# First loads of three phases issued in the phase before them, in a two-layer recurrent decoder step

## Chip, cores and metric

One core of one Trainium2 chip runs one program. The metric is the device time of one execution in microseconds (us), lower is better.

## What is computed

One inference step of a decoder trunk with two layers, for a prompt of 2048 tokens and a sample group of 8 sequences of 8 tokens, width 1024, all in float32. Cut from the reference:

```python
# every layer
x <- x + gate(c) * RMSNorm_post(mixer(RMSNorm_pre(x) * (1 + scale(c)) + shift(c)))

def mixer_ab(h, ...):      # layer 0: GLA (4 heads) and retention (4 heads)
    gq, gk, gv, gz, glr, rq, rk, rv, rz = split(h @ w_in)
    log_a = log_sigmoid(glr @ w_gate_up + b_gate) / GLA_TAU
    q_r, k_r = rotary(rq), rotary(rk)
    o, s = chunked_gated_linear_attn(q, k, v, log_g, s0)     # S = diag(exp(g)) S + k v^T
    return (norm(o) * silu(z)) @ w_out, s

def mixer_c(h, ...):       # layer 1: gated delta rule, 8 heads
    qkv, z, b_raw, a_raw = split(h @ w_in)
    qkv = silu(causal_conv_of_width_4(qkv))
    q, k = l2norm(q), l2norm(k)
    o, s = chunked_gated_delta(q, k, v, sigmoid(b_raw), log_g, s_delta)
    return (rms_norm(o) * silu(z)) @ w_out, s
```

The outputs are the new tokens and the new states.

## The kernel before

The program is four phases one behind the other. Names of a phase's tiles begin with its short name: `inab` (first projection, with the adaLN conditioning, `phase_in_ab`), `mixab` (layer 0's recurrence and output projection, `phase_mix_ab`), `inc` (second projection and convolution, `phase_in_c`), `mixc` (delta rule and last output projection, `phase_mix_c`). A phase ends with `ph.end()`: the semaphores are cleared and all engines meet at a barrier, so nothing of a phase starts before the last work of the one before is done. Between phases the results go through arrays in device memory (`tmp_qk`, `tmp_v`, `tmp_z`, `tmp_dec` to `mixab`; `tmp_x` to `inc`; `tmp_qkv`, `tmp_z`, `tmp_col`, `tmp_brow` to `mixc`).

Each engine has an instruction stream written out by hand: PE (matmuls), ACT, DVE, POOL, and SP, which only issues DMAs. DMAs are issued from SP's queue and from ACT's. Every wait is a semaphore count. The order of the work around the change is thus the order of the code.

The two projections go in four blocks of 512 prompt tokens and the 64 sample tokens. A block has its normed, transposed tokens in one of two operand rooms: `keep` and a second one of 16 KB per partition, which is `inab_h` in `inab` and `raw_next` in `inc` (allocated in `mixab`, where the class `Early`, L1218, fills it with layer 1's first block; `inc` uses it for blocks 0 and 2). `outputs` (L739 in `inab`) stores a block's results from SP; the last things on SP's queue in `inab` are the stores of block 3 and of the sample (L751 to L768).

The mix phases go in 16 tiles of 128 tokens and one of the sample. Each loads a tile two ahead (`load_tile`, L1382 and L2357) into buffers 0 and 1. SP loads tile 0 first of all, behind the barrier, then the constant tables (`load_tables`, L172, one DMA for each table, from one array in which they lie side by side), then tile 1 and the weights. PE waits for the tables (`tab_in`) at the start of every phase, since the identity matrix for transposes is one of them. In `mixc` ACT issues the load of tile 0's `qkv` (L2579) and SP everything else; ACT's second step waits for the norm weights `gn` (L2381), the last of SP's first loads.

At the tail of `mixab`, layer 1's conditioning is worked out beside the sample tile: `Cond.pair` (L260) multiplies 2 MB pieces of `w_ada`, which ACT loads into a ring of three buffers `cw` (L228), and `Early` squares and norms token tiles (L1234 to L1249).

`inc` converts its 33 weight units of 128 columns while block 0 runs, with the class `Weights` (L530): ACT's queue loads a unit in f32 to one of two stages (L547), ACT rounds it to f16 (`hi`, L556) and POOL subtracts for the remainder (`lo`, L562); each conversion first issues the load of the next unit. A block has 36 groups: 24 of convolution channels, 8 of `z`, 4 of the small columns. A z group needs four units at once. PE multiplies a group into one of four banks, ACT copies it out (`evac`, L1996), DVE convolves (L2085 to L2091), ACT stores. In group g of block 0 ACT and POOL also convert unit 4 + g:

```python
                if first:
                    weights.hi(act, AHEAD + g)      # L2020; AHEAD = 4
```

so unit 27, which the first z group needs, comes in slot 23. The convolution's coefficients (`conv_c`) are loaded by SP as rows (L1886), transposed by PE (L2155) and copied by ACT (L1977) before the first product.

## Time and profile before

| | |
|---|---|
| runs (3), us | 2666.85, 2667.93, 2664.86; median 2666.85 |
| profiled execution, us | 2668.84, span 2667.1 |
| mean granted TensorE clock | 0.965 of full speed |
| PE busy | 2482.0 us (93%) |
| DVE busy | 1320.2 us (50%) |
| ACT busy | 926.3 us (35%) |
| POOL busy | 796.3 us (30%) |
| DMA | 270.37 MB, mean 101 GB/s |

The device time holds a little more than the span, which runs from the first to the last instruction. An engine's busy share is a mean over phases with different limits. SP's and ACT's DMA issues, marked q in the rows, don't count as busy. A row of a timeline gives the start, the duration, the engine, the line and operation, the tile written and those read, the count, and in brackets the idle time ahead with what ended it. The clock of a window is a share of 2.4 GHz, and 0.50 is the lower level of 1.2 GHz.

### The profile page before, as it was taken

To read this page: it belongs to the slowest core of one execution; us is meant where nothing else is said; L and a number is where in the kernel's file an instruction comes from. 1 tells how busy PE (TensorE), PEld (TensorE's weight loads), DVE (VectorE), ACT (ScalarE), POOL (GpSimd) and SP (SyncE) were. 2 spreads that over 40 slices of the span, in tenths; PEclk is the share of its full clock that TensorE was granted. 3 is DMA by queue.
4 is the path that set the end of the run, shared out by engine and by line. 5 is a ranking of instruction groups with operands and counts; after the bars stand their busy time and mean duration, and the time that the engine had idled before them with its cause. 6 is when DMAs were issued, how large, how long until landed. Compare 5 with 4: busy or idle time off the path is not lost. (4 is left out here: it accounts for less than half of the span.)

```text
span 2667.1 us, 53838 instructions
## 1 busy us (share of the span) xinstructions
PE 2482.0 (93%) x21052; PEld 1495.8 (56%) x21052; DVE 1320.2 (50%) x2927; ACT 926.3 (35%) x2664; POOL 796.3 (30%) x848
## 2 busy tenths in 40 slices
PE   7999999997899986989999999985899999999998
PEld 2444444444566632434444444455788787887876
DVE  3412112111687743981643626424666566665666
ACT  3534242322111113432322322234445454554541
POOL 2531001021111103551010000005555556465564
PEclk8999999998999996989999999997999999999998
DMA  8451212033544543542121111116513222231213
GB/s 294 132 157 48 83 45 75 32 117 124 209 146 157 173 162 114 162 135 77 64 72 52 64 52 52 56 48 174 136 58 107 63 81 89 65 105 57 81 46 92
DMA packets 256585, 270.37 MB, mean 101 GB/s; under 512 B 31223, under 2 KB 189959, under 8 KB 256378
## 3 DMA queue, kind: packets, MB, share of 16 engines
q1 hardware_dynamic: 184858, 217.28, 25.1%
q10 hardware_dynamic: 71520, 50.13, 6.7%
q8 instruction: 155, 2.54, 0.4%
q14 instruction: 52, 0.43, 0.1%
HBM read 180.00 MB, written 87.36 MB: 100 GB/s over the span
## 5 line engine op out<-in xcount | busy, mean ns | idle before, releaser
L613 PE MATMUL inc_b<-raw_next,inc_w_hi 128*128 128x512 bf16 (+1 forms) x768 | 229.7, 381 | 0.5 <-ACT inc_taps L1977 0.5
L613 PE MATMUL inc_b<-keep,inc_w_hi 128*128 128x512 bf16 (+1 forms) x768 | 228.5, 379 | 0.0
L613 PE MATMUL inab_b<-inab_wt,keep 128*128 128x512 f16 x768 | 167.1, 379 | 4.3 <-POOL inab_wt L562 4.1
L613 PE MATMUL inab_b<-inab_wt,inab_h 128*128 128x512 f16 x768 | 166.4, 379 | 0.0
L1131 PE MATMUL mixab_y<-keep,mixab_oT_hi 128*128 128x512 f16 x512 | 152.5, 379 | 7.9 <-DVE mixab_f_y L1211 6.2
L2089 DVE SCALAR_TENSOR_TENSOR inc_acc<-inc_ub,inc_taps,inc_acc 128x512 f32<-128x512 f32 x192 | 152.1, 792 | 6.8
L2085 DVE COPY inc_ub<-inc_halo 128x3 f32<-128x3 f32 x96 | 21.5, 223 | 252.6 <-ACT inc_ub L1996 252.6
L613 PE MATMUL inc_b<-raw_next,inc_w_lo 128*128 128x512 bf16 x384 | 146.1, 381 | 0.0
L613 PE MATMUL inc_b<-keep,inc_w_lo 128*128 128x512 bf16 x384 | 145.6, 379 | 0.0
L1996 ACT ACTIVATE inc_ub<-inc_b 128x512 f32<-128x512 f32 x96 | 57.0, 594 | 252.6 <-PE inc_b L613 252.6
L613 PEld LDWEIGHTS inab_b<-inab_wt,keep 128*128 128x128 bf16 (+1 forms) x768 | 74.8, 98 | 95.6 <-issue 6.0
L613 PEld LDWEIGHTS inab_b<-inab_wt,inab_h 128*128 128x128 bf16 (+1 forms) x768 | 75.1, 98 | 90.9 <-issue 1.1
L613 PEld LDWEIGHTS inc_b<-raw_next,inc_w_hi 128*128 128x128 f16 x768 | 75.2, 98 | 90.0 <-issue 1.3
L613 PEld LDWEIGHTS inc_b<-keep,inc_w_hi 128*128 128x128 f16 x768 | 74.9, 98 | 89.3
L885 ACT ACTIVATE inab_vz<-inab_b 128x512 f32<-128x512 f32 x66 | 39.4, 596 | 243.1 <-PE inab_b L613 224.3
L398 DVE TENSOR_SCALAR keep<-keep,inab_rstd 128x1024 f32<-128x1024 f32 (+1 forms) x13 | 12.1, 932 | 202.3 <-POOL inab_rstd L393 202.3
L2480 POOL TENSOR_TENSOR mixc_levels<-mixc_BT,mixc_tab 128x512 f32<-128x512 f32 (+1 forms) x82 | 110.2, 1375 | 1.5 <-DVE mixc_BT L2774 1.5
L562 POOL TENSOR_TENSOR inc_w_lo<-inc_stage,inc_w_hi 128x1024 f16<-128x1024 f32 (+1 forms) x33 | 78.0, 2364 | 84.0 <-ACT inc_w_hi L556 84.0
L613 PE MATMUL inc_b<-inc_w_hi,raw_next 128*128 128x512 f16 (+2 forms) x400 | 85.7, 313 | 17.0 <-POOL inc_w_lo L562 17.0
L525 POOL TENSOR_TENSOR keep<-keep 128x1024 f16<-128x1024 f32 x12 | 27.7, 2309 | 239.3 <-ACT keep L520 239.3
L1131 PE MATMUL mixc_y<-mixc_w_hi,mixc_oT_hi 128*128 128x512 f16 x256 | 97.4, 381 | 0.0
L1131 PE MATMUL mixc_y<-mixc_w_lo,mixc_oT_hi 128*128 128x512 f16 x256 | 97.1, 379 | 0.0
(523 smaller groups left out, 6108.5 us busy)
## 6 DMA issues: line engine op xcount, KB each, us to landing
tmp_qkv<-inc_so SPq DMA_DIRECT2D x96, 256.0 KB, 2.0
mixc_qkv<-tmp_qkv SPq DMA_DIRECT2D x15, 1536.0 KB, 7.7
inc_stage<-in_w_in_c ACTq DMA_DIRECT2D x32, 512.0 KB, 4.5
inab_stage<-in_w_in_ab ACTq DMA_DIRECT2D x24, 512.0 KB, 4.1
mixab_cw<-in_w_ada ACTq DMA_DIRECT2D x6, 2048.0 KB, 14.6
inab_wt<-in_w_ada SPq DMA_DIRECT2D x10, 1024.0 KB, 14.5
keep<-in_x_prompt SPq DMA_DIRECT2D x16, 512.0 KB, 4.2
tmp_v<-inab_vz SPq DMA_DIRECT2D x32, 256.0 KB, 3.9
```

Source lines behind the costliest of these rows:

```text
L398: dve.tensor_scalar(self.xn[0:n, :], self.x[par][0:n, :], self.rs[0:n, par:par + 1], None, ALU.mult).then_inc(self.xnd, 1)
L525: pool.tensor_tensor(room[1][:, :, col:col + n], self.hf[:, :, 0:n], room[0][:, :, col:col + n], ALU.subtract).then_inc(self.lo_done, 1)
L562: eng.tensor_tensor(self.place(1, c0, m), self.stage[u % self.slots][:, :, 0:m], self.place(0, c0, m), ALU.subtract).then_inc(self.lo_done, 1)
L613: last = nc.tensor.matmul(dst, lhs(a, k), rhs(b, k), start=(k == 0 and i == 0), stop=(k == KT - 1 and i == len(PASSES) - 1))
L885: act.activation(vz[:, j % 4, :], src[:], ACT.Copy if j < (2 * TPB if n == BLK else 1) else ACT.Silu).then_inc(evac, 1)
L1131: last = self.nc.tensor.matmul(self.banks[half][0:n, :], (self.oT_hi, self.oT_lo)[a][:, h, 0:n], self.w[b][:, h, half * 512:(half + 1) * 512],
L1996: act.activation(ub[g % 2][:, CONV - 1:], src[:], ACT.Copy).then_inc(evac, 1)
L2085: chain.link(dve.tensor_copy(u_[:, 0:CONV - 1], h_))
L2089: chain.link(dve.scalar_tensor_tensor(a_v, win(i), taps[:, c, i:i + 1], a_v, ALU.mult, ALU.add))
L2480: pool.tensor_tensor(BTm[w][0:n], BT[0:n, :, 0:HB], bc(tv[f"pick{w}"][0:n].unsqueeze(1), [n, H, HB]), ALU.mult).then_inc(btm_ready, 1)
```

## The change

1. `load_tables` joins tables that lie side by side into one DMA (`runs`). The three first ones (sel, sel_s, ident) go to a tile `tab0` that lives as long as the program, and later phases take them from there. So PE no longer waits for a table at the start of `mixab` and `inc`, and in `mixc` only for what DVE copies out of them.
2. `raw_next` lives over the whole program and is the second operand room of `inab` too. When PE has finished block 3, SP loads `mixab`'s tile 0 into it, ahead of the sample's stores. In `mixab` tile 0 is taken from there, and tile 2 is loaded at the start.
3. One of the three `cw` buffers is a tile `stage_next` that lives on into `inc`. Once PE has used its last piece of `w_ada`, SP loads the first two weight units of `inc` and the convolution rows into it. In `inc` it is the room of the weight stages, of the rows and of the store buffers; nothing of these is loaded behind the barrier.
4. In block 0 of `inc`, slots 3 and 10 (`TWICE`) convert two units each. The sample's operand gets a room of its own.
5. In block 3 of `inc`, SP loads `mixc`'s `qkv` of tile 0 (1.57 MB) into `raw_next`, which block 2 was the last to use, ahead of block 3's stores. ACT's load at the start of `mixc` is gone.

The diff, cut:

```diff
 def load_tables(eng, sem, dst, names, table_d):
     at = 0
+    for c0, w in runs(names):
+        eng.dma_start(dst[:, at:at + w], table_d[:, c0:c0 + w]).then_inc(sem, 16)
+        at += w
+def runs(names):
+    out = []
     for n in names:
         c0, w = TABLE[n]
-        eng.dma_start(dst[:, at:at + w], table_d[:, c0:c0 + w]).then_inc(sem, 16)
-        at += w
+        if out and sum(out[-1]) == c0:
+            out[-1] = (out[-1][0], out[-1][1] + w)
+        else:
+            out.append((c0, w))
+    return out
...
@@ phase_in_ab, SP
         outputs(nb - 1, BLK, TPB, [])
         rot_load(nb, NS)
+        sp.wait_ge(mm, G * nb)
+        for i in range(4):
+            sp.wait_ge(vz_out[i], 16 + 16 * TPB)
+        sp.dma_start(pre[0].rearrange("p (g n) -> p g n", g=8), io["qk0"][:, :, 0:P].rearrange("g p n -> p g n")).then_inc(pre_in, 16)
+        sp.dma_start(pre[1], io["v0"][0:P, :]).then_inc(pre_in, 16)
+        sp.dma_start(pre[2], io["z0"][0:P, :]).then_inc(pre_in, 16)
+        sp.dma_start(pre[3], io["dec0"][:, 0, :]).then_inc(pre_in, 16)
         outputs(nb, NS, 1, [])
+        sp.wait_ge(pre_in, 64)
...
@@ phase_mix_ab, SP
-        load_tile(sp, 0, 0, P)
+        sp.sem_inc(tile_in[0], 64)
         load_tables(sp, tab_in, tab, names, io["table"])
         load_tile(sp, 1, 1, P)
...
+        load_tile(sp, 2, 0, P)
...
-        turn(0, 0, 0, P, P)
...
         fin.load_sample(sp, io["x_sample"], io["gate_s"][0], 0, gate_in)
+        stages, rows_c = in_c_stages(stage_next)
+        sp.wait_ge(cond.mm, 4)
+        for unit, stage in enumerate(stages):
+            sp.dma_start(stage, io["w_in_c"].rearrange("(k p) n -> p k n", p=P)[:, :, unit * P:(unit + 1) * P]).then_inc(next_in, 16)
+        for i in range(3):
+            sp.dma_start(rows_c[32 * i:32 * i + CONV, :], io["conv_c"][:, i * D:(i + 1) * D]).then_inc(next_in, 16)
...
@@ phase_mix_ab, PE
-        pe.wait_ge(tab_in, 16 * len(names))
...
@@ phase_in_c
+    TWICE = (3, 10)
+    units_at = [range(AHEAD + g + sum(t < g for t in TWICE), AHEAD + g + 1 + sum(t <= g for t in TWICE)) for g in range(G)]
...
-        for i in range(3):
-            sp.dma_start(rows[32 * i:32 * i + CONV, :], io["conv_c"][:, i * D:(i + 1) * D]).then_inc(rows_in, 16)
+        sp.sem_inc(rows_in, 48)
+        for i in range(2):
+            sp.sem_inc(weights.stage_in[i], 16)
...
+        sp.wait_ge(mm, G * (nb - 1))
+        for i in range(2):
+            sp.wait_ge(so_out[i], 16 * (1 + NCH // 2))
+        sp.dma_start(first_chunks(io), io["qkv1"][:, :, 0:P].rearrange("c p n -> p c n")).then_inc(pre_in, 16)
         outputs(nb - 1, BLK, [])
...
@@ phase_in_c, POOL, and ACT alike with weights.hi
-            weights.lo(pool, AHEAD + g)
+            for u in units_at[g]:
+                weights.lo(pool, u)
...
@@ phase_in_c, ACT
-        for unit in range(weights.slots - 1):
-            weights.load(act, unit)
-        weights.hi(act, 0)
+        weights.hi(act, 0, False)
...
@@ phase_mix_c
-    qkv = [ph.sb(f"qkv{i}", [P, NCH, P]) for i in range(2)]
+    qkv = [first_chunks(io), ph.sb("qkv1", [P, NCH, P])]
...
+        sp.sem_inc(tile_in[0], 16)
...
-        act.dma_start(qkv[0][:], io["qkv1"][:, :, 0:P].rearrange("c p n -> p c n")).then_inc(tile_in[0], 16)
...
-        pe.wait_ge(tab_in, 16)
...
-            pe.wait_ge(tile_in[par], 32 * (half + 1))
+            pe.wait_ge(tile_in[par], 32 * (half + 1) if not isinstance(t, int) or t else 16)
```

Where the instructions stand. SP from the end of block 3 in `inab` to the first loads of `mixab`, before:

```order
L778 DMA tmp_z<-inab_vz 128x512 x8
L785 DMA inab_cs<-in_rot 128x2x64
L751 DMA tmp_qk<-inab_u 128x2x64
...
L756 DMA tmp_dec_s<-inab_decay_s 128x32
...
L763 DMA tmp_qk<-inab_r 128x2x64
L768 DMA tmp_v<-inab_vz 64x512 x2
L768 DMA tmp_z<-inab_vz 64x512 x2
L133 UNCONDITIONAL_BRANCH
L1392 UNCONDITIONAL_BRANCH
L1384 DMA mixab_qk<-tmp_qk 128x8x128
L1385 DMA mixab_v<-tmp_v 128x1024
L1386 DMA mixab_z<-tmp_z 128x1024
```

and now:

```order
L816 DMA raw_next<-tmp_qk 128x8x128
L817 DMA raw_next<-tmp_v 128x1024
L818 DMA raw_next<-tmp_z 128x1024
L819 DMA raw_next<-tmp_dec 128x8
L769 DMA tmp_qk<-inab_u 128x2x64
...
L774 DMA tmp_dec_s<-inab_decay_s 128x32
...
L781 DMA tmp_qk<-inab_r 128x2x64
L786 DMA tmp_v<-inab_vz 64x512 x2
L786 DMA tmp_z<-inab_vz 64x512 x2
L133 UNCONDITIONAL_BRANCH
L1428 UNCONDITIONAL_BRANCH
L176 DMA mixab_tab<-in_table 128x256
```

The four loads of tile 0 have moved from behind the phase's end to ahead of the sample's stores, and the joined tables (L176) come first behind it.

SP from the tail of `mixab` to the start of `inc`, before:

```order
L1156 DMA mixab_f_gate<-tmp_gate_s 64x512
L1438 DMA out_gla_sample<-mixab_Ss 128x8x128 x2
L1438 DMA out_ret_sample<-mixab_Ss 128x8x128
...
L1162 DMA tmp_x_s<-mixab_f_x 64x512 x2
...
L177 DMA inc_tab<-in_table 128x128 x3
L1886 DMA inc_so<-in_conv_c 4x1024 x3
L1887 DMA inc_alog<-in_a_log_c 128x8
L1888 DMA inc_alog<-in_dt_bias_c 128x8
```

and now:

```order
L1182 DMA mixab_f_gate<-tmp_gate_s 64x512
L1475 DMA stage_next<-in_w_in_c 128x8x128 x2
L1477 DMA stage_next<-in_conv_c 4x1024 x3
L1480 DMA out_gla_sample<-mixab_Ss 128x8x128 x2
L1480 DMA out_ret_sample<-mixab_Ss 128x8x128
...
L1188 DMA tmp_x_s<-mixab_f_x 64x512 x2
...
L176 DMA inc_tab<-in_table 128x256
L1938 DMA inc_alog<-in_a_log_c 128x8
...
```

The convolution rows and two weight units (which ACT's queue loaded in `inc` before) stand ahead of the sample's state stores.

ACT in block 0 of `inc` (L547 and L558 are the same load, L556 and L567 the same conversion, L1996 and L2051 the copy out of a bank, L1989 and L2044 the store buffer's activation), slots 2 to 4 before:

```order
L547 DMA inc_stage<-in_w_in_c 128x8x128
L556 ACTIVATE inc_w_hi<-inc_stage 128x8x128
L1996 ACTIVATE inc_ub<-inc_b 128x512
L1989 ACTIVATE inc_so<-inc_acc 128x512
L547 DMA inc_stage<-in_w_in_c 128x8x128
L556 ACTIVATE inc_w_hi<-inc_stage 128x8x128
L1996 ACTIVATE inc_ub<-inc_b 128x512
L1989 ACTIVATE inc_so<-inc_acc 128x512
L547 DMA inc_stage<-in_w_in_c 128x8x128
L556 ACTIVATE inc_w_hi<-inc_stage 128x8x128
```

and now:

```order
L558 DMA stage_next<-in_w_in_c 128x8x128
L567 ACTIVATE inc_w_hi<-stage_next 128x8x128
L2051 ACTIVATE inc_ub<-inc_b 128x512
L2044 ACTIVATE stage_next<-inc_acc 128x512
L558 DMA stage_next<-in_w_in_c 128x8x128
L567 ACTIVATE inc_w_hi<-stage_next 128x8x128
L558 DMA stage_next<-in_w_in_c 128x8x128
L567 ACTIVATE inc_w_hi<-stage_next 128x8x128
L2051 ACTIVATE inc_ub<-inc_b 128x512
L2044 ACTIVATE stage_next<-inc_acc 128x512
L558 DMA stage_next<-in_w_in_c 128x8x128
L567 ACTIVATE inc_w_hi<-stage_next 128x8x128
```

Slot 3 holds two loads and two conversions ahead of the copy out of the next bank.

## Rows read from the trace of the kernel before

**Rows 1.** Waits of PE over the whole run: waiter, releaser: us in total, times, longest.

```profile
PE mixc_B L3005 <- DMA mixc_qkv<-tmp_qkv: 27.8, 1, 27.8
PE inc_b L613 <- POOL inc_w_lo L562: 17.0, 2, 11.0
PE inc_t L2155 <- DMA inc_so<-in_conv_c: 14.1, 1, 14.1
PE mixab_kv L1689 <- DMA mixab_tab<-in_table: 14.0, 1, 14.0
```

**Rows 2.** Timeline of SP, end of the first phase: start, us, what (q: issue).

```profile
630.16 0.38 SPq L751 DMA_DIRECT2D tmp_qk<-inab_u  x1
...
644.56 0.39 SPq L1384 DMA_DIRECT2D mixab_qk<-tmp_qk  x1
```

**Rows 3.** Timeline of POOL, SP, PE, DVE at the mix phase's start.

```profile
647.49 0.52 POOL L1453 MEMSET mixab_S<- 128x512 f32 x1
...
646.57 3.39 SPq L177 DMA_DIRECT2D mixab_tab<-in_table  x7
...
653.24 1.12 PE L1689 MATMUL mixab_kv<-mixab_tab,mixab_qk 128*128 128x128 f32 x4 [13.95 <-DMA mixab_tab<-in_table]
...
656.45 1.12 DVE L1554 TENSOR_TENSOR mixab_sc<-mixab_be,mixab_tab 64x512 f32<-64x512 f32 x2 [20.49 <-PE mixab_bo L1699]
```

**Rows 4.** Timeline of PE and ACT at the mix phase's tail.

```profile
992.36 5.30 PE L260 MATMUL mixab_y<-mixab_cw,mixab_cT 128*9 128x512 f32 x16 [3.13 <-DMA mixab_cw<-in_w_ada]
...
993.51 1.06 ACT L1239 ACTIVATE mixab_exn<-mixab_v 128x1024 f32<-128x1024 f32 x1 [5.02 <-DMA mixab_v<-tmp_x]
```

**Rows 5.** Window in that tail: us, busy per engine, clock, DMA share, GB/s.

```profile
988.00:992.00 4.00, 1.23 (x6) 0.14 (x2) 2.62 (x4) 0.49 (x1) 0.00 (x0) 1.00 1.05 413
```

**Rows 6.** Timeline of SP, ACT, POOL, PE at the second projection's start.

```profile
1043.17 1.67 SPq L177 DMA_DIRECT2D inc_tab<-in_table  x3
...
1046.46 1.06 ACT L556 ACTIVATE inc_w_hi<-inc_stage 128x1024 f16<-128x1024 f32 x1 [13.07 <-DMA inc_stage<-in_w_in_c]
...
1047.67 2.12 POOL L562 TENSOR_TENSOR inc_w_lo<-inc_stage,inc_w_hi 128x1024 f16<-128x1024 f32 x1 [4.96 <-ACT inc_w_hi L556]
...
1051.85 1.03 PE L613 MATMUL inc_b<-raw_next,inc_w_hi 128*128 128x512 bf16 x2 [0.47 <-ACT inc_taps L1977]
```

**Rows 7.** Timeline of DVE, ACT, POOL in its block 0.

```profile
1079.44 3.29 DVE L2089 SCALAR_TENSOR_TENSOR inc_acc<-inc_ub,inc_taps,inc_acc 128x512 f32<-128x512 f32 x2
...
1084.44 1.54 DVE L2089 SCALAR_TENSOR_TENSOR inc_acc<-inc_ub,inc_taps,inc_acc 128x512 f32<-128x512 f32 x2
...
1083.75 0.63 ACT L1989 ACTIVATE inc_so<-inc_acc 128x512 f32<-128x512 f32 x1 [3.61 <-DVE inc_acc L2091]
...
1179.50 2.58 POOL L562 TENSOR_TENSOR inc_w_lo<-inc_stage,inc_w_hi 128x1024 f16<-128x1024 f32 x1
...
1189.63 2.55 POOL L562 TENSOR_TENSOR inc_w_lo<-inc_stage,inc_w_hi 128x1024 f16<-128x1024 f32 x1 [2.50 <-ACT inc_w_hi L556]
```

**Rows 8.** Windows round PE's longest wait there.

```profile
1195.00:1198.00 3.00, 3.00 (x9) 1.06 (x7) 0.00 (x0) 0.00 (x0) 0.00 (x0) 0.50 0.01 3
1198.00:1201.00 3.00, 3.00 (x15) 1.32 (x13) 0.00 (x0) 0.34 (x1) 0.00 (x0) 0.94 0.00 0
```

**Rows 9.** Timeline of SP, DVE and ACT at the delta phase's start.

```profile
1804.82 10.56 SPq L2359 DMA_DIRECT2D mixc_col<-tmp_col  x1
...
1810.23 1.77 DVE L2756 COPY mixc_levels<-mixc_tab 128x512 f32<-128x512 f32 x5 [15.45 <-DMA mixc_tab<-in_table]
...
1842.09 0.21 ACT L2593 ACTIVATE mixc_ebl<-mixc_seg 128x8 f32<-128x8 f32 x1 [3.64 <-DMA mixc_gn<-in_g_norm_c]
```

**Rows 10.** Window of the same stretch.

```profile
1820.00:1824.00 4.00, 3.77 (x21) 3.58 (x19) 0.00 (x0) 2.73 (x12) 3.84 (x5) 0.63 1.21 290
```

**Rows 11.** DMA issues: what, queue, KB each, us to landing.

```profile
mixc_qkv<-tmp_qkv SPq DMA_DIRECT2D x15, 1536.0 KB, 7.7
inc_stage<-in_w_in_c ACTq DMA_DIRECT2D x32, 512.0 KB, 4.5
```

More of the change, by code:

```diff
@@ L945, in _ @@
             cond.add(dve, n)
-        dve.wait_ge(tab_in, 16 * len(names))
+        dve.wait_ge(tab_in, 16 * len(runs(names)))
         for g in range(2):
@@ L1029, in _ @@
         cond.pair(pe, 2)
-        pe.wait_ge(tab_in, 16 * len(names))
+        pe.wait_ge(tab_in, 16 * len(runs(names)))
         pe.wait_ge(small_in, 32)
@@ L1542, in _ @@
     def _(dve):
-        dve.wait_ge(tab_in, 16 * len(names))
+        dve.wait_ge(tab_in, 16 * len(runs(names)))
         dve.wait_ge(init, 1)
@@ L1748, in _ @@
         for t in range(2):
-            tile(t, t, 0)
+            tile(t, (2, 1)[t], 0)
         with pe.Fori(1, nt // 2) as i:
@@ L2019, in groups @@
                 if first:
-                    weights.hi(act, AHEAD + g)
+                    for u in units_at[g]:
+                        weights.hi(act, u)
         groups(0, [(4 + tc, P) for tc in range(4)], True)
@@ L2243, in _ @@
         turned(2)
+        pe.wait_ge(tab_in, 16 * len(runs(names)))
         pe.wait_ge(g_ready, 1)
```

69 lines of the change are left out of this document (44 added, 25 removed).

## The prediction

> **What bounds the kernel now.** The table of engines puts the matmul engine (PE) at 2482.0 of 2667.1 us, so first I read PE's waits, grouped by what ended them [rows 1]. The reader is to see four groups: 27.8 us for the delta phase's first tile, 14.1 for the convolution rows and 14.0 for the tables, each at a phase's start, and 17.0 in two waits for POOL's half of a weight unit. They are 73 us, but much of the three is the barrier and the end of the phase before, so I then read the timelines of the engines round each place for what would end that wait next, and the windows for bandwidth and clock. Elsewhere PE hardly waits; the change touches no inner loop but the second projection's block 0.
>
> **The change part by part.** (Gains positive; "now" is the change.)
>
> *Start.* Three table issues become one, on SP's queue ahead of the tokens on which ACT and then everything waits. Seven table issues took 3.39 us [rows 3], 0.48 each, so two fewer: **+0.9**. Bounds 0.3 (the tokens' landing limits) and 2 (the second set, seven issues to one, helps too).
>
> *Into the mix phase.* The tile-0 load (1.57 MB) now stands behind block 3's last product and ahead of the sample's first store. That store isn't issued before 630.16, and the next phase's first issue is at 644.56 [rows 2]; four issues of about half a microsecond fit before the store, and the landing has ten: cost nothing. Had the store no slack, the 2 us of issues would show. PE's tile and tables are in place at the barrier, so it starts at 644.6, not at 653.24 [rows 3]. From its start to DVE's first mask took 656.45 - 653.24 = 3.2 us [rows 3], which gives 647.8. DVE also needs POOL's zeroing, ended 647.49 + 0.52 = 648.0 [rows 3], and the tables: two issues from 644.56 end at 645.5; the seven ended at 649.96 and PE was released 3.3 later, so they are there by 648.8 at the latest. DVE starts at 648.1 to 648.8 instead of 656.45, 7.6 to 8.4: **+8.0** (6.8 if the tile stores and loads collide).
>
> *Tail of the mix phase.* SP now fetches 1.05 MB of weights and 48 KB of convolution rows exactly when ACT fetches the last 2 MB of the conditioning weights and a token tile. PE waits 3.13 us for the former and ACT 5.02 for the latter, and both are on the path, while the DMA engines are full: 413 GB/s, share 1.05 [rows 4, 5]. 1.1/0.413 = 2.7 us later at that rate; rows of 512 B usually run nearer the 290 GB/s of [rows 10], 3.8. I take **-3.2**; ends 0 (they land after the 2 MB) and -4.5.
> The Trainium skill (DMA: Bandwidth & Descriptors, Queues, rings and completion order) has each DMA engine alternate between the queues packet by packet. With as many rows in a packet on either queue, the 512 B rows would take a fifth of the bytes while the 2 KB rows of the conditioning weights run, 0.5 MB, and cost 1.2 us; the sum would be 2 us better. No run here shows it.
>
> *Into the second projection.* The first conversion starts at 1046.46, released by its weights, POOL's half at 1047.67 takes 2.12, and PE's first product starts at 1051.85 behind the taps [rows 6]. Now weights and rows are there: SP's first issue is at 1043.17 [rows 6], one table issue (0.45) and three semaphore increments later it is about 1044.0. ACT 1044.0 to 1045.1, POOL to 1047.3, the taps' transposes (about 2 us) beside them. PE starts at about 1047.4: **+4.4** (3.5 to 6.0). The next wait is POOL's low half.
>
> *Block 0 of the second projection.* Each of 24 channel groups converts one weight unit, PE runs ahead and then needs unit 27 for its first z group. POOL does that unit in slot 23 (1189.63, 2.55 [rows 7]) and PE starts behind it after 11.0 us [rows 1]. Now unit 27 is done in slot 21, whose POOL instruction ended at 1179.50 + 2.58 = 1182.1 [rows 7]: 10.1 us earlier. Against it stand two slots with one unit more each. (a) A POOL instruction of this kind lengthens what DVE does: two DVE instructions took 3.29 us under it and 1.54 without [rows 7], 1.75 each. DVE sets the pace here (POOL and ACT wait each slot), so two more cost 3.5. (b) ACT's second conversion waits for its unit, fetched only at the slot's start: 4.5 us [rows 11], plus 1.04 to convert, less the 1.6 of the first, 4.0 later; ACT has 3.61 of slack before the next store [rows 7], so some 0.5 to 1 comes through, 1.5 for both. Unit 27 is thus done 10.1 - 5.0 = 5.1 earlier, with slots before it moved alike: **+5.2**. The second wait, 17.0 - 11.0 = 6.0 [rows 1], for unit 31, disappears (that unit has the two slots' lead and PE is only 5 earlier): **+6.0**. After the first the granted clock is 0.50, the 1.2 GHz level: 9 matmuls in 3 us where the next 3 us hold 15 [rows 8], about 3 us lost over the six. PE still waits 5.7 there and restarts cold; the second restart, after the shorter wait of 6.0 (half of it taken), goes: **+1.7**. Together **+12.9** (7 if they cost the double and a restart is not saved, 19 if nothing).
> Of the lock the Trainium skill (SBUF — State Buffer, Who interferes with whom) says that whoever of DVE and GpSimd has the shared ports keeps them for its whole instruction and the other fully blocks. By it each added POOL instruction could cost its full 2.58 rather than 1.75; the gain would be 1.7 smaller. The row decides for 1.75.
>
> *Block 3 of the second projection.* The 1.57 MB load of the delta phase's tile 0 lies between block 2's and block 3's stores on SP's queue. Behind it stand only channel stores, for which ACT has two buffers and PE four output banks ahead of ACT; a load like it lands in 7.7 us [rows 11]: nothing. Without that cover it would cost up to 7.7.
>
> *Into the delta phase.* PE now needs only tables and tile 0. But what starts the second step is different: ACT at 1842.09 waited 3.64 us for the norm weights, the last of SP's first loads, and one 20 KB issue there took 10.56 us because the queue was full [rows 9]. Chain: queue full, bytes drained at 290 GB/s [rows 10], last load, ACT. ACT's competing load of 1.57 MB is gone: 1.57/0.290 = 5.4 us less, 1.57/0.413 = 3.8. The engines' own chain moves more: PE waits only for DVE's copies of the tables, ended 1810.23 + 1.77 = 1812.0 or a bit before [rows 9], instead of 1817.32 (27.8 in [rows 1]), so 5.3 to 7.3, and ACT was already ready at 1842.09 - 3.64 = 1838.45. **+5.0**; ends 3.7 and 7.3. The next wait stays the norm weights.
>
> **Sum.** 0.9 + 8.0 - 3.2 + 4.4 + 12.9 + 0 + 5.0 = 28.0. The profiled run was 2668.84, so 2640.8; the runs' median of 2666.85 is 2.0 below it, hence **2639**. About 0.2%, 5.3 us, is what a measurement of this kernel can tell from no change.
>
> **Rivals.**
> 1. *The doubled slots are free* (DVE and ACT absorb them): unit 27 done 10 us earlier, PE's wait is below 1 us, the clock stays up (3.0 more, ten cold product pairs). For: ACT idles 3 us in a slot. Against: DVE doesn't. 12.9 + 4.8 + 3.0: about **2631**. Chance 0.12.
> 2. *The next wait takes most.* The boundaries are won only in part (tables land beside new tile loads; the norm weights still come last since the queue is held by its own count of descriptors, not by bytes, so the delta phase gains 0) and the tail's fetch costs 4.5. 5 + 3 + 1.3 less: about **2649**. For: the 10.56 of [rows 9]. Chance 0.18.
> 3. *Whole-instruction blocking* in the doubled slots: two POOL instructions at 2.58 each, and ACT's stall doubled: 3.2 less, about **2642**. Chance 0.10. The row of 3.29 speaks against.
> 4. *Slower.* The fetch at the mix phase's tail in 512 B rows shares the engines with loads on the path, and the sample's state stores stand behind it on SP's queue. It decides from the point where it costs more than the other 31 us: the 1.1 MB would have to run at 35 GB/s. At 25 GB/s it would take 44 us and give about **2680**. Units of 0.5 MB of this very shape land in 4.5 us [rows 11], 115 GB/s for one by itself, so it is unlikely. Chance 0.04.
> 5. *It doesn't do what it says*: the early loads wait for a semaphore that comes only at the phase's end and land no earlier. Then the three boundaries give nothing, the start its 0.9, block 0 its 12.9 and the tail -3.2: about **2656**; with block 0 at its low end of 7 it would be 2662, no change. For: SP waits for the stores and the products before each. Against: SP stood idle at each place in the trace [rows 2]. Chance 0.04 and 0.03.
>
> **How the numbers follow.** Forecast as summed 0.49. Rivals 1 to 3 and the first half of 5 are faster by more than 5.3 us too: 0.49 + 0.12 + 0.18 + 0.10 + 0.04 = 0.93; same 0.03, slower 0.04. The terms' low ends all together (0.3 + 6.8 - 4.5 + 3.5 + 7 + 3.7 = 16.8) give 2650, the high ends (2 + 8.4 - 0 + 6 + 19 + 7.3 = 42.7) 2624; both together are rare, rivals 1 to 3 lie inside. Range **2626 to 2652**.
>
> **What would show it.** In the profile after: PE starts the mix phase within 1 us of SP's first issue and DVE at about 648; PE's wait for the conditioning weights near 6 us instead of 3.1; first product of the second projection 4.4 nearer to the barrier; POOL's waits in block 0 one of 5 to 6 us instead of 17.0 in two, and DVE's channels in the two doubled slots 1.7 us longer; in the delta phase ACT's wait still ended by the norm weights, 5 us nearer to SP's first issue. I am wrong if the tail's wait grows past 8, if block 0 shows a wait above 8, or if block 3 shows a PE wait of its own.

## The result and the profile after

| | before | change |
|---|---|---|
| runs, us | 2666.85, 2667.93, 2664.86, 2661.52; median 2665.86 | 2643.09, 2636.45, 2635.51, 2641.47; median 2638.96 |
| profiled execution, us (span) | 2668.84 (2667.1) | 2643.09 (2641.3) |
| ratio, 95% interval | | 0.9892 [0.9876, 0.9909] |
| mean granted clock | 0.965 | 0.969 |

A second measurement on another occasion (e5 below) gave 0.9885 [0.9865, 0.9904]. The change is 27 us faster, and the forecast was 2639. Its profiled execution was the slowest of its four, so in what follows profiles are compared with profiles and medians with medians. Since a right sum can hide wrong terms, each term is checked against its own stretch.

The waits of PE in the change: waiter, releaser, us in total, times, longest.

```profile
PE mixc_B L3059 <- DVE mixc_levels L2811: 25.0, 1, 25.0
...
PE inc_t L2210 <- SPq L1935: 8.1, 1, 8.1
...
PE inc_b L624 <- POOL inc_w_lo L573: 6.9, 2, 5.0
...
PE mixab_y L271 <- DMA mixab_cw<-in_w_ada: 5.3, 1, 5.3
...
PE mixab_kv L1731 <- SPq L1430: 5.0, 1, 5.0
```

The 27.8, 14.1 and 14.0 us of [rows 1] are 25.0, 8.1 and 5.0, and the latter two are released by SP's first increments behind the barrier, so nothing is waited for there but the barrier. The 17.0 us for POOL's halves are 6.9. The size of one entry was not foreseen: PE's wait at the delta phase's start has hardly shrunk. It is ended by DVE's copies, as forecast, but they end later (line 2811 of the changed kernel, as all line numbers from here on are the changed kernels' own).

The start of the mix phase, timelines of SP, POOL and DVE in the change (answers to [rows 2, 3]):

```profile
623.55 2.06 SPq L816 DMA_DIRECT2D raw_next<-tmp_qk  x1
...
632.83 0.40 SPq L769 DMA_DIRECT2D tmp_qk<-inab_u  x1
...
647.01 0.84 SPq L176 DMA_DIRECT2D mixab_tab<-in_table  x2
...
649.85 0.53 POOL L1496 MEMSET mixab_S<- 128x512 f32 x1
...
650.48 1.12 DVE L1597 TENSOR_TENSOR mixab_sc<-mixab_be,mixab_tab 64x512 f32<-64x512 f32 x2 [11.85 <-POOL mixab_S L1496]
```

The four loads are issued at 623.55 to 627.2, the sample's first store at 632.83, so they are covered. DVE starts behind POOL's zeroing (650.38) and not behind the tables: from SP's first issue it is 3.5 us instead of 11.9.

The mix phase's tail, timelines of PE and ACT and the window, in the change ([rows 4, 5]):

```profile
989.39 5.82 PE L271 MATMUL mixab_y<-mixab_cw,mixab_cT 128*9 128x512 f32 x16 [5.33 <-DMA mixab_cw<-in_w_ada]
...
990.75 1.06 ACT L1265 ACTIVATE mixab_exn<-mixab_v 128x1024 f32<-128x1024 f32 x1 [7.42 <-DMA mixab_v<-tmp_x]
```

```profile
984.00:988.00 4.00, 0.07 (x2) 0.00 (x0) 3.78 (x4) 0.00 (x0) 0.00 (x0) 0.88 1.07 396
```

PE waits 5.33 us for the 2 MB instead of 3.13, ACT 7.42 for its tokens instead of 5.02.

The start of the second projection, SP, ACT, POOL, PE ([rows 6]):

```profile
1036.80 0.35 SPq L176 DMA_DIRECT2D inc_tab<-in_table  x1
...
1037.29 1.06 ACT L567 ACTIVATE inc_w_hi<-stage_next 128x1024 f16<-128x1024 f32 x1 [10.13 <-SPq L1937]
...
1038.50 2.12 POOL L573 TENSOR_TENSOR inc_w_lo<-stage_next,inc_w_hi 128x1024 f16<-128x1024 f32 x1 [2.04 <-ACT inc_w_hi L567]
...
1041.15 0.63 PE L624 MATMUL inc_b<-raw_next,inc_w_hi 128*128 128x512 f16 x1 [1.97 <-POOL inc_w_lo L573]
```

Block 0 of it: timelines of DVE and POOL in the doubled slot 3 (the first two rows), of DVE in the doubled slot 10, and of PE at the first z group, and the windows behind ([rows 7, 8]):

```profile
1074.39 1.72 DVE L2141 COPY inc_ub<-inc_halo 128x3 f32<-128x3 f32 x1 [0.49 <-ACT inc_ub L2051]
...
1073.94 2.14 POOL L573 TENSOR_TENSOR inc_w_lo<-stage_next,inc_w_hi 128x1024 f16<-128x1024 f32 x1 [1.59 <-ACT inc_w_hi L567]
...
1115.24 1.71 DVE L2141 COPY inc_ub<-inc_halo 128x3 f32<-128x3 f32 x1 [1.22 <-ACT inc_ub L2051]
...
1178.52 0.59 PE L624 MATMUL inc_b<-inc_w_hi,raw_next 128*128 128x512 f16 x1 [4.98 <-POOL inc_w_lo L573]
```

```profile
1180.00:1183.00 3.00, 3.00 (x11) 1.19 (x10) 2.93 (x3) 1.28 (x2) 2.12 (x1) 0.73 0.70 165
...
1183.00:1186.00 3.00, 3.00 (x15) 1.37 (x14) 2.77 (x6) 1.72 (x3) 0.50 (x2) 1.00 0.42 123
```

In slot 3 DVE waits 0.49 us for ACT and then its small copy takes 1.72 instead of 0.16, 2.05 us in all. The copy started 0.45 us behind POOL's added instruction and ended with it (1076.11 and 1076.08). In slot 10 DVE waits 1.22 us for ACT, and the copy takes 1.71. PE's wait is 4.98, and the clock is back to full after 1183.

The delta phase's start, SP, DVE, POOL, PE, ACT ([rows 9]):

```profile
1781.79 6.92 SPq L2415 DMA_DIRECT2D mixc_col<-tmp_col  x1
...
1785.72 5.61 DVE L2811 COPY mixc_levels<-mixc_tab 128x512 f32<-128x512 f32 x5 [14.05 <-DMA mixc_tab<-in_table]
...
1785.82 2.08 POOL L2504 TENSOR_TENSOR mixc_seg<-mixc_seg,mixc_col 128x1024 f32<-128x1024 f32 x1 [4.49 <-DMA mixc_tab<-in_table]
...
1791.43 1.94 PE L3059 MATMUL mixc_B<-tab,raw_next 128*128 128x128 f32 x8 [24.99 <-DVE mixc_levels L2811]
...
1813.47 0.21 ACT L2648 ACTIVATE mixc_ebl<-mixc_seg 128x8 f32<-128x8 f32 x1 [1.43 <-DMA mixc_gn<-in_g_norm_c]
```

SP's full-queue issue took 6.92 us instead of 10.56, and the second step (ACT at 1813.47) waits 1.43 for the norm weights instead of 3.64. New is that DVE's five copies took 5.61 us instead of 1.77, beside two POOL instructions.

Which of the two paths bounds this start is shown by the chain of work that ended last, followed back from the last instruction (start, us, what). Its part here is, before:

```profile
1832.64 9.42 DMA mixc_gn<-in_g_norm_c
```

and in the change:

```profile
1780.36 5.34 DMA mixc_tab<-in_table
1785.72 5.62 DVE mixc_levels L2811 x5
```

Before, it goes through the norm weights. In the change it goes through the tables, DVE's copies and PE, and the norm weights are not on it, though ACT still waits 1.43 us for them. The same holds for the second profiles of either kernel.

To set terms apart I cut every profile at the same events. Columns: us between the events; "again" are second profiles of the same kernels (e11, e5).

| from ... to | before | again | change | again | forecast |
|---|---|---|---|---|---|
| start ... last rotary load of the first phase (SP) | 620.1 | 619.2 | 622.8 | 620.5 | -0.9 |
| ... first mask of the mix phase (DVE) | 36.3 | 36.3 | 27.7 | 27.6 | -8.0 |
| ... last `w_ada` load (ACT) | 328.1 | 331.5 | 328.9 | 331.4 | 0 |
| ... last mean of the mix phase (DVE) | 50.8 | 46.4 | 49.9 | 50.0 | +3.2 |
| ... first product of the second projection (PE) | 16.4 | 16.7 | 12.0 | 11.6 | -4.4 |
| ... SP's first issue in the delta phase | 750.4 | 748.7 | 738.3 | 738.3 | -12.9 |
| ... ACT's second step | 39.8 | 39.9 | 34.0 | 33.9 | -5.0 |
| ... end | 825.0 | 828.9 | 827.8 | 827.7 | 0 |
| span | 2667.1 | 2667.6 | 2641.3 | 2640.9 | -28.0 |

Stretches that the change hardly touches differ by 1 to 4 us between profiles of one kernel (620.1 and 619.2, 328.1 and 331.5, 825.0 and 828.9). The change's touched stretches repeat to 0.4, but two of before's don't (50.8 and 46.4, 750.4 and 748.7). ACT's second step is a mark of convenience, and what is won there need not last. Further marks, in us, with DVE's last instruction of a channel (L2147 in the change) for block 0 of the second projection and ACT's first instruction of the fourth step (L2648) for the delta phase:

| profile | first channel of block 0, behind PE's first product | last channel of block 0 | first channel of block 1 | fourth step, behind SP's first issue |
|---|---|---|---|---|
| before, again | 15.2, 15.2 | 140.4, 140.4 | 203.8, 203.7 | 127.3, 130.7 |
| change, again | 16.1, 16.6 | 147.4, 146.8 | 191.3, 191.3 | 122.7, 122.7 |
| e1 | 16.2 | 141.4 | 204.4 | 123.1 |
| e2 | 14.7 | 144.9 | 190.0 | 124.2 |
| e3 | 16.3 | 146.4 | 190.4 | 122.4 |
| e4 | 16.2 | 147.6 | 191.7 | 121.9 |
| e6 | 15.9 | 147.4 | 191.4 | 121.2 |
| e7 | 16.4 | 146.6 | 190.8 | 116.2 |
| e8 | 16.1 | 147.8 | 185.6 | 123.0 |
| e9 | 16.5 | 148.0 | 185.9 | 116.3 |
| e10 | 15.1 | 146.7 | 184.6 | 120.0 |

The last mark is the least steady: e7, e9 and e10 have the same delta phase, and 116.2, 116.3 and 120.0.

### The profile page after: what moved, and what is told of

Its sections match the earlier page's. It is cut to its first block and busy times, and to the rows that moved or that the text cites. A ratio compares the mean times of both kernels' runs of the same rounds, so it can differ in the third digit from the quotient of the medians.

```text
span 2641.3 us, 53763 instructions
## 1 busy us (share of the span) xinstructions
PE 2476.6 (94%) x20987; PEld 1497.5 (57%) x21052; DVE 1328.6 (50%) x2927; ACT 926.9 (35%) x2664; POOL 796.3 (30%) x848
## 5 line engine op out<-in xcount | busy, mean ns | idle before, releaser
L624 PE MATMUL inc_b<-raw_next,inc_w_hi 128*128 128x512 f16 (+1 forms) x760 | 228.1, 381 | 3.2 <-POOL inc_w_lo L573 2.0
L624 PE MATMUL inab_b<-inab_wt,raw_next 128*128 128x512 f16 x768 | 166.4, 379 | 0.0
L2051 ACT ACTIVATE inc_ub<-inc_b 128x512 f32<-128x512 f32 x96 | 57.0, 594 | 251.1 <-PE inc_b L624 247.0
L624 PE MATMUL inc_b<-raw_next,inc_w_lo 128*128 128x512 bf16 x368 | 140.2, 381 | 0.0
L624 PE MATMUL inc_b<-keep,inc_w_lo 128*128 128x512 bf16 x366 | 138.7, 379 | 0.0
L624 PEld LDWEIGHTS inab_b<-inab_wt,raw_next 128*128 128x128 bf16 (+1 forms) x768 | 75.2, 98 | 90.8 <-issue 1.1
L409 DVE TENSOR_SCALAR keep<-keep,inab_rstd 128x1024 f32<-128x1024 f32 (+1 forms) x13 | 12.1, 932 | 202.6 <-POOL inab_rstd L404 202.6
L536 POOL TENSOR_TENSOR raw_next<-keep,raw_next 128x1024 f16<-128x1024 f32 x12 | 28.0, 2336 | 243.0 <-ACT raw_next L531 243.0
L536 POOL TENSOR_TENSOR keep<-keep 128x1024 f16<-128x1024 f32 x12 | 27.7, 2309 | 240.6 <-ACT keep L531 240.6
L1157 PE MATMUL mixab_y<-keep,mixab_oT_lo 128*128 128x512 f16 x256 | 97.5, 381 | 0.0
```

Of the source, the lines that this page charges most:

```text
L536: pool.tensor_tensor(room[1][:, :, col:col + n], self.hf[:, :, 0:n], room[0][:, :, col:col + n], ALU.subtract).then_inc(self.lo_done, 1)
L624: last = nc.tensor.matmul(dst, lhs(a, k), rhs(b, k), start=(k == 0 and i == 0), stop=(k == KT - 1 and i == len(PASSES) - 1))
L1157: last = self.nc.tensor.matmul(self.banks[half][0:n, :], (self.oT_hi, self.oT_lo)[a][:, h, 0:n], self.w[b][:, h, half * 512:(half + 1) * 512],
L2051: act.activation(ub[g % 2][:, CONV - 1:], src[:], ACT.Copy).then_inc(evac, 1)
```

## The experiments

All ratios are to the kernel before on the same chip, with 95% intervals; e1 to e4, e5 to e8 and e9 to e11 ran together.

### e1: no doubled slots

```diff
-    TWICE = (3, 10)
+    TWICE = ()
```

> The change without the two doubled conversion slots (one unit per slot, as before). Forecast's theory (each slot is 5.06 us, the two doubled ones cost 5.0 of it back, the second wait and restart vanish): 12.9 us slower than the change, about 2652 us; PE's waits for POOL's half in block 0 are again about 17 us in two. Rival (the doubled slots cost nothing or almost): 16 to 19 us slower. Rival (the gain of the second projection comes from the early weights, not from the slots): under 4 us slower.

2655.34 us, 0.9951 [0.9937, 0.9964]. Its waits of PE:

```profile
PE inc_b L624 <- POOL inc_w_lo L573: 19.9, 3, 11.9
```

The stretch of the second projection is 751.4 us, 13.1 more than the change's 738.3, and 1.0 and 2.7 more than in the two profiles of before. The 19.9 are the first unit's 2.0 and two waits of 11.9 and 6.0, where before had 11.0 and 6.0. By the mark at block 1, too, it is 13.1 (204.4 and 191.3). The slots are the whole gain of that phase behind its start; 12.9 was forecast. The medians lie 16.4 us apart (2655.34 and 2638.96, of different occasions), the size that the rival gave for slots that cost nothing. With intervals some 8 us wide they can't decide, but DVE's rows in slots 3 and 10 can: the slots do cost it time.

### e2: the fetch of the tail taken back

```diff
@@ phase_mix_ab, SP
-        sp.wait_ge(cond.mm, 4)
-        for unit, stage in enumerate(stages):
-            sp.dma_start(stage, ...).then_inc(next_in, 16)
-        for i in range(3):
-            sp.dma_start(rows_c[32 * i:32 * i + CONV, :], ...).then_inc(next_in, 16)
@@ phase_in_c, SP, then ACT
-        sp.sem_inc(rows_in, 48)
-        for i in range(2):
-            sp.sem_inc(weights.stage_in[i], 16)
+        for i in range(3):
+            sp.dma_start(rows[32 * i:32 * i + CONV, :], ...).then_inc(rows_in, 16)
...
+        for unit in range(weights.slots - 1):
+            weights.load(act, unit)
-        weights.hi(act, 0, False)
+        weights.hi(act, 0)
```

> The change without the fetch of two weight units and convolution rows in the mix phase's tail; they are loaded behind the barrier as before. Forecast's theory (the fetch costs 3.2 us in the tail and gains 4.4 behind the barrier): 1.2 us slower than the change, about 2640. Rival from the change's trace (the fetch makes PE wait 5.3 instead of 3.1 us, but the later arrival lets POOL's two small instructions of the early norm miss DVE's 2.28 us instruction, which had stretched them from 0.19 and 0.54 to 1.23 and 2.46, so that the tail in all is 1.0 us shorter, not longer): 5 to 6 us slower, about 2645, with PE's wait back at 3.1, the two POOL instructions stretched again and ACT's wait for them 4.0.

2638.62 us, 0.9889 [0.9874, 0.9904]: no slower than the change. PE's wait is back at 3.64 (3.13 and 3.10 before), and POOL's pair is not stretched, so the rival (which took its 1.0 us from the one profile of before) falls. PE and POOL in the tail of e2:

```profile
985.35 5.76 PE L271 MATMUL mixab_y<-mixab_cw,mixab_cT 128*9 128x512 f32 x16 [3.64 <-DMA mixab_cw<-in_w_ada]
...
994.74 0.19 POOL L1269 TENSOR_SCALAR mixab_e_ms<-mixab_e_ss 128x1 f32<-128x1 f32 x1 [6.12 <-ACT mixab_exn L1265]
...
995.01 0.54 POOL L1271 TENSOR_TENSOR mixab_e_rs<-mixab_e_ms,mixab_f_mhalf 128x1 f32<-128x1 f32 x1
```

By stretches the tail is 46.7 us against the change's 49.9 and 50.0 (3.2 to 3.3 shorter), and the way from the last mean to the first product 16.9 against 12.0 and 11.6 (4.9 to 5.3 longer). By these two stretches the fetch is worth 1.6 to 2.1 us, but block 0 takes part of it back: in e2 block 1 begins 190.0 us behind the first product, in the six profiles with these slots and the fetch 190.4 to 191.7. From the last `w_ada` load to SP's first issue in the delta phase e2 takes 798.7 us, the change 800.2 and 799.8, e3, e4, e6 and e7 798.0 to 802.0. So neither the stretches to the phase's end nor the runs, whose intervals are 8 us wide, show a gain.

Part of the 3.2 is not the fetch's. In both profiles of the change POOL's third pair is stretched (1.58 us for 0.54), in e2 none is. The profiles with the fetch and no stretched pair (e3, e7, e8) have tails of 49.1, 48.6 and 48.9 us, those without the fetch and without a stretched pair (e2 and the second of before) 46.7 and 46.4: the fetch costs 1.9 to 2.7.

### e3: the delta phase's tile loaded behind the barrier

```diff
@@ phase_in_c, SP
-        sp.wait_ge(mm, G * (nb - 1))
-        for i in range(2):
-            sp.wait_ge(so_out[i], 16 * (1 + NCH // 2))
-        sp.dma_start(first_chunks(io), io["qkv1"][:, :, 0:P]...).then_inc(pre_in, 16)
@@ phase_mix_c, SP, ACT, PE
-        sp.sem_inc(tile_in[0], 16)
+        act.dma_start(qkv[0][:], io["qkv1"][:, :, 0:P]...).then_inc(tile_in[0], 16)
-            pe.wait_ge(tile_in[par], 32 * (half + 1) if not isinstance(t, int) or t else 16)
+            pe.wait_ge(tile_in[par], 32 * (half + 1))
```

> The change without the early load of the delta phase's first tile; ACT's queue loads it behind the barrier as before. Forecast's theory (the queue drains 1.57 MB later, the norm weights land later): 5.0 to 5.8 us slower, about 2644, the first ACT instruction of the second step released by the norm weights again. Rival (PE's own start, 3.9 us held back in the change by DVE's copies that run beside POOL's decay instructions, takes the place of the load): 2 us slower or less.

2643.88 us, 0.9912 [0.9898, 0.9925]. SP and ACT in its delta phase:

```profile
1778.01 0.35 SPq L2419 DMA_DIRECT2D mixc_col<-tmp_col  x1
...
1780.59 9.81 SPq L2410 DMA_DIRECT2D mixc_col<-tmp_col  x1
...
1816.69 0.21 ACT L2644 ACTIVATE mixc_ebl<-mixc_seg 128x8 f32<-128x8 f32 x1 [3.78 <-DMA mixc_gn<-in_g_norm_c]
```

From SP's first issue (1778.01) to the second step it is 38.7 us, 4.7 more than in the change, and the norm weights release it. The full-queue issue takes 9.81 instead of 6.92. Up to the second step that is the forecast's mechanism at its size: a load on ACT's queue lengthens SP's. Whether by its bytes or by its number of descriptors no run tells apart. But the loss doesn't last in this profile: the fourth step comes at 122.4 us, in the change at 122.7, and the whole phase takes 861.2 us against the change's 861.8 and 861.6. The profiled run was the fastest of this kernel; the medians of the runs, of different occasions, are 4.9 us apart, with overlapping intervals. So the early load is shown to win 4.7 us at the second step, and not shown to win them at the end.

### e4: the mix phase's tile loaded behind the barrier

```diff
@@ phase_in_ab, SP
-        sp.wait_ge(mm, G * nb)
-        for i in range(4):
-            sp.wait_ge(vz_out[i], 16 + 16 * TPB)
-        sp.dma_start(pre[0]...)   # and pre[1], pre[2], pre[3]
@@ phase_mix_ab, SP
-        sp.sem_inc(tile_in[0], 64)
+        load_tile(sp, 0, 2, P)
...
+        sp.wait_ge(tile_in[0], 64)
         load_tile(sp, 2, 0, P)
```

> The change with the mix phase's tile 0 loaded behind the barrier (ahead of the two joined table loads), all else kept. Theory A (of the 8.6 us at this boundary the tables' joining and the persistent identity are worth over half): 3 to 4.5 us slower than the change, about 2642.5, PE released by the tile some 6.5 us behind SP's first issue. Theory B (the early tile is the whole gain, since tile and tables land together at the drained rate): 7 to 8.6 us slower, about 2647.

2648.47 us, 0.9926 [0.9912, 0.9939]. SP and PE at the phase's start:

```profile
642.82 0.39 SPq L1412 DMA_DIRECT2D raw_next<-tmp_qk  x1
...
650.17 1.12 PE L1724 MATMUL mixab_kv<-tab,raw_next 128*128 128x128 f32 x4 [12.30 <-DMA raw_next<-tmp_dec]
```

PE is released 7.35 us behind SP's first issue, where before it took 8.7 with seven tables and the tile. The stretch to the first mask is 34.7 us, 7.0 longer than in the change and 1.7 shorter than before. Theory A falls: of 8.6 us at this boundary the early tile gives 7.0, the joined tables by themselves 1.7. The edit also holds the load of tile 2 back until tile 0 is there. The medians are 9.5 us apart; the profile shows 7.0 at this boundary and 1.3 to 1.4 more in the tail, where a pair of POOL's is stretched (2.46), and the rest stays open.

### e5: the change again

> The change itself, beside the next three, as their base: 0.9892 of the kernel before, within its interval.

2639.21 us (2633.62 to 2643.57, 6 runs), 0.9885 [0.9865, 0.9904]. The runs of this kernel spread over 10 us.

### e6: DVE's copies ahead of POOL's first decay instructions

```diff
@@ phase_mix_c, POOL
         pool.wait_ge(tab_in, 16)
+        pool.wait_ge(y_init, 1)
```

> The change, with POOL's first decay instructions in the delta phase waiting for DVE's five copies of a table. In the change's trace the copies took 5.61 us beside POOL's instructions, 1.77 before. Theory (POOL and DVE block one another, and the second step is bound by the norm weights): the copies take 1.8 again, PE's first matmul of the phase comes 3.9 us earlier, and the run is no faster (under 0.5 us), since ACT's second step still waits for the norm weights. Rival (PE's start bounds the phase): 3 to 4 us faster. Rival (the copies are slow for the DMAs that run meanwhile): the copies still take over 4 us.

2641.02 us, 0.9898 [0.9879, 0.9917]. DVE, PE and ACT at the delta phase's start:

```profile
1786.11 1.77 DVE L2812 COPY mixc_levels<-mixc_tab 128x512 f32<-128x512 f32 x5 [14.15 <-DMA mixc_tab<-in_table]
...
1787.98 1.94 PE L3060 MATMUL mixc_B<-tab,raw_next 128*128 128x128 f32 x8 [21.25 <-DVE mixc_levels L2812]
...
1815.03 0.21 ACT L2649 ACTIVATE mixc_ebl<-mixc_seg 128x8 f32<-128x8 f32 x1 [5.89 <-DMA mixc_gn<-in_g_norm_c]
```

The copies take 1.77 us again with the same DMAs under way, and PE starts 8.2 us behind SP's first issue instead of 11.9. The medians don't fall: the norm weights release the second step, with 5.89 us of idle ahead now, and 35.2 us behind SP's first issue instead of 34.0. So the two engines block one another. But it was on the path: the chain that ended last, which went through these copies in the change, goes through the norm weights in e6, and the fourth step comes at 121.2 us instead of 122.7. The slow copies thus cost some 1.5 us there and no more, since the norm weights stood close behind. That is less than the runs can show, and little beside the spread of this mark (121.9 to 124.2 in the kernels with the change's delta phase).

### e7: the same, and the norm weights early

```diff
@@ phase_mix_c, SP
+        sp.dma_start(gn[:], io["g_norm_c"]...).then_inc(gn_in, 16)
         load_rows(1, 1, P)
         load_tile(1, 1, P)
...
         sp.dma_start(fin.gate[:], io["gate_p"][1]).then_inc(gate_in, 16)
-        sp.dma_start(gn[:], io["g_norm_c"]...).then_inc(gn_in, 16)
```

> As the one before, and the norm weights are loaded ahead of the delta phase's second tile and weights instead of last. Theory (norm weights bound, the engines' own chain is next): ACT's second step is released 5.4 us earlier, about 5 us faster than the change, 2634. Rival (the weights of the output projection, which ACT converts ahead of the second step, are next): 1 to 2 us faster only, with an ACT wait for them.

2634.13 us, 0.9875 [0.9853, 0.9897]. ACT and SP:

```profile
1777.15 0.35 SPq L2425 DMA_DIRECT2D mixc_col<-tmp_col  x1
...
1806.27 0.25 ACT L2649 ACTIVATE mixc_ebl<-mixc_seg 128x8 f32<-128x8 f32 x1
```

The second step starts with no wait, 29.1 us behind SP's first issue instead of 34.0: 4.9 us, as expected, and the median is 5.1 below the change's (the intervals overlap). At the fourth step it is 6.5 us ahead of the change (116.2 and 122.7), and the chain goes through the tables and copies again. So two paths bounded the phase's start side by side: moving PE alone gives some 1.5 us there, moving it together with the norm weights 6.5. The norm weights alone were not tried; the change's trace leaves them 1.43 us at most.

### e8: three doubled slots

```diff
-    TWICE = (3, 10)
+    TWICE = (3, 8, 14)
```

> The change with three doubled conversion slots (3, 8, 14) instead of two. Theory (each doubled slot moves unit 27 one slot of 5.06 us earlier and costs 2.0 to 2.5 us): PE's wait ahead of the first z group falls from 5.0 to about 2.3, 2.7 us faster than the change, up to 5 if the clock stays up. Rival (a doubled slot now costs as much as it gives, since ACT's stalls add up): no change, wait still 4 to 5.

2636.32 us, 0.9881 [0.9859, 0.9902]. Its waits of PE, second projection's start and block 0:

```profile
PE inc_t L416 <- DVE keep L409: 2.9, 1, 2.9
...
PE inc_b L624 <- POOL inc_w_lo L573: 2.0, 2, 1.6
```

The wait for unit 27 is all but gone (0.4 us), and PE waits 2.9 us for DVE's `keep` instead. The stretch of the second projection is 730.9 us, 7.4 shorter than the change's, but e9 with the same slots has 734.4. Block 0 itself gives 5.7 us in e8 and 5.4 in e9 (block 1 begins at 185.6 and 185.9 instead of 191.3): 5.0 of wait and some of the cold restart. The rest lies in blocks that the edit doesn't touch. That is the upper end of what was expected, and the marks say why: from the first channel of block 0 to the last DVE takes 125.2 us in e1 with no doubled slot, 131.3 and 130.2 with two (change, again), and 131.7 and 131.5 with three (e8, e9). The two slots thus cost 6.1 and 5.0 us, the three only 6.5 and 6.3. From one channel to the next, slots 3, 8 and 14 of e8 take 2.2, 2.2 and 2.1 us more than the same slots of e1, slot 10 in the second profile of the change 2.9. The medians differ by 2.9 us; the runs' spread hides the rest.

### e9, e10: all together, and the same without the fetch

e9 has the edits of e7 and e8, e10 those and e2's.

> The change with three doubled slots, the norm weights early and POOL's decay instructions behind DVE's copies. Theory (the gains are at different places on the path and add): 5 us from the delta phase's start and 3 to 7 from block 0, 8 to 12 faster than the change, about 2630. Rival (the clock gives part back, or the sum is under the noise): 4 to 6 faster.

> As e9, without the fetch in the mix phase's tail. From the two traces the fetch costs 3.2 us in the tail and gains 4.9 behind the barrier: 1.7 us slower than e9, within what can be told. Rival (the fetch isn't worth anything): equal or faster.

e9: 2635.76 us, 0.9873 [0.9856, 0.9889]. e10: 2633.38 us, 0.9869 [0.9852, 0.9885]. They have the lowest ratios of all, 3 to 6 us below the change, but e7's 0.9875 is no worse within the intervals. It is less than the 8 to 12 expected for e9; the marks have 5.4 us in block 0 and 6.4 at the fourth step, near 12, and e9's profiled span is 8.4 to 8.8 us below the change's. In e9's profile the tail of the mix phase is 51.5 us and the second projection 734.4; in e10's they are 47.4 and 729.7. POOL in e9's tail shows a stretched instruction again:

```profile
1000.39 1.79 POOL L1269 TENSOR_SCALAR mixab_e_ms<-mixab_e_ss 128x1 f32<-128x1 f32 x1 [7.27 <-ACT mixab_exn L1265]
```

Whether the fetch is worth having stays open: e2 and e10 say that it gives nothing one can tell, as the rival for e10 had it.

### e11: the kernel before, again

> The kernel before, a second profile. Its first profile showed POOL's second pair of small instructions of the early norm stretched to 1.23 and 2.46 us under a DVE instruction, PE cold after it. If that belongs to this kernel's order it is there again, with the stretch from the mix phase's conditioning products to its last mean 50.8 us long; if it was chance of that run, the pair takes 0.19 and 0.54 and the stretch is about 4 us shorter.

2669.38 us. POOL and DVE in the tail, in the first profile of before, and then in the second:

```profile
1001.96 1.23 POOL L1243 TENSOR_SCALAR mixab_e_ms<-mixab_e_ss 128x1 f32<-128x1 f32 x1 [6.29 <-ACT mixab_exn L1239]
...
1003.27 2.46 POOL L1245 TENSOR_TENSOR mixab_e_rs<-mixab_e_ms,mixab_f_mhalf 128x1 f32<-128x1 f32 x1
...
1001.91 1.23 DVE L1667 TENSOR_TENSOR mixab_Ss<-mixab_Ss,mixab_dec_s 128x1024 f32<-128x1024 f32 x1
...
1003.06 2.28 DVE L1635 TENSOR_TENSOR mixab_vm<-mixab_v,mixab_tab 64x2048 f32<-64x2048 f32 x1
```

```profile
1004.28 0.19 POOL L1243 TENSOR_SCALAR mixab_e_ms<-mixab_e_ss 128x1 f32<-128x1 f32 x1 [6.22 <-ACT mixab_exn L1239]
...
1004.56 0.54 POOL L1245 TENSOR_TENSOR mixab_e_rs<-mixab_e_ms,mixab_f_mhalf 128x1 f32<-128x1 f32 x1
...
1005.07 1.22 DVE L1667 TENSOR_TENSOR mixab_Ss<-mixab_Ss,mixab_dec_s 128x1024 f32<-128x1024 f32 x1
```

In the first profile POOL's two instructions, of 128 x 1 elements, start just as DVE's 1.23 and 2.28 us ones do and take 1.23 and 2.46 us; in the second they start 0.8 us ahead of DVE's and take 0.19 and 0.54. The stretch is 50.8 us in the one and 46.4 in the other, of the same program. So it was chance of that run, and 46.4 is the base against which the fetch must be held, in profiles whose own pairs are not stretched either.

## Why the prediction was right

*Start, +0.9.* SP reaches block 0's first store at 113.27 instead of 114.42, 1.15 earlier. At the phase's end none of it is shown: the mark there lies at 620.1 and 619.2 before and at 618.4 to 622.8 in the changed kernels. The fall of the clock told in the last section takes some 1.7 us in some of them; the rest is open.

*Into the mix phase, +8.0.* Measured 8.6, the early tile being 7.0 of it (e4). The step "DVE also needs POOL's zeroing" was the binding one, at its low end. The cover named for the early load held.

*Tail, -3.2.* The stretch grew by 3.5 against the second profile of before, but 1 us of it is the change's own stretched pair; with no pair stretched on either side it is 1.9 to 2.7. The waits say the same: PE's is 5.2 to 5.6 us in the nine profiles with the fetch and 3.1 to 3.6 in the four without, ACT's 7.4 to 7.7 and 5.0 to 5.5. So the term was some 1 us too large. Against the only profile known then it is +0.9, which looks like a failed term until the collision of POOL and DVE is seen. The packet-by-packet rule of the Trainium skill (DMA: Bandwidth & Descriptors, Queues, rings and completion order), by which I had worked out an estimate of 1.2 us for equally many rows in a packet, comes out too low here: the waits grew by about 2.1 and 2.4 us on the mean. All 1.1 MB at the window's 396 GB/s would be 2.8, so the delay lies between the two.

*Into the second projection, +4.4.* Measured 4.4 to 5.1 at the first product. PE's first product (1041.15) follows POOL's low half, which ended at 1040.62, as said. What the forecast left out is that PE's first product is not what paces block 0: DVE's first channel comes 16.1 to 16.6 us behind it instead of 15.2, and in e1, which has the early start but no doubled slot, block 1 begins 0.6 to 0.7 us later behind it than before. So much of the gain is given back.

*Block 0, +12.9.* Measured 12.1 between the first profiles and 10.4 between the second over the whole phase, 12.5 and 12.4 to the first channel of block 1, and 13.1 by e1. Within it: the wait is 4.98 where 5.7 was said, unit 31's is gone. The other 2.0 of the 6.9 is the phase's first unit. The two doubled slots, taken as 5.0, cost DVE 6.1 and 5.0 us, and not evenly: 2.1 for slot 3 in either profile, the rest for slot 10. The part that comes through from ACT's late unit, taken as 0.5 to 1, is 0.49 and 1.22. The Trainium skill's lock (SBUF — State Buffer, Who interferes with whom) would have had up to 2.58 for the POOL instruction, and I had let a row decide for 1.75. That was a misreading: the row's 2.58 us were themselves lengthened (the same instruction takes 2.12 in [rows 6]), and how long DVE is held depends on when the two start. In slot 3 DVE's copy ended with POOL's instruction and lost 1.56 us rather than 2.14 because it started later; the trace agrees with the Trainium skill. The price of 3.5 for both was near all the same.

*Block 3, 0.* No PE wait there, and the stretch isn't longer.

*Into the delta phase, +5.0.* Measured 5.8 and 6.0 at the second step, 4.7 by e3, and 4.6 and 8.0 at the fourth step. That the norm weights bounded the start before, and that the early load brings them forward, e3 and the chain of before show. What the forecast had wrong is what comes next: "the engines' own chain moves more, 5.3 to 7.3", and "the next wait stays the norm weights". PE started 11.9 us behind SP's first issue instead of 15.1, 3.1 less, because DVE's copies now coincide with POOL's decay instructions: before, those waited for the tile. ACT was still ready 1.4 us ahead of the norm weights, but the chain that ended last now runs through the copies and PE. By e6 this cost some 1.5 us at the fourth step, little enough to leave the sum right.

The rivals: the doubled slots were not free (rival 1), the next wait didn't take most (2), the doubled slots cost DVE 5.0 to 6.1 us and not 3.2 more than the 5.0 forecast (3), though DVE was held until POOL's instruction ended, the tail's fetch cost under a tenth of what would have made it slower (4), and the loads land where the code puts them (5). By the second profiles the stretches give 8.6 + 5.1 - 3.6 + 10.4 + 6.0 = 26.5, and the medians differ by 26.9. That the forecast came to 2639 and the median to 2638.96 is luck: the tail was priced too high, the first mask too low, part of the start is given back in block 0, and untouched stretches differ by up to 4 us. The range, too, was put together unevenly: the low and high ends of the terms gave 2650 and 2624 from the median, and 2652 and 2626, which was stated, from the profiled run.
